# Seven 2x2-block products in place of eight for the last two blocks of each quarter of the down projection

## The chip, the cores and the metric

The kernel runs on one core of a Trainium2 chip. The metric is the device time of one execution in microseconds (us). The core's engines run side by side and meet at semaphores: TensorE (PE, with its weight loads as PEld), VectorE (DVE), ScalarE (ACT), GpSimd (POOL), and the queue of SyncE (SP), which here only issues transfers.

## The reference

One layer of a transformer-like trunk for 256 tokens of width 2048, in float32: two token mixers side by side (retention, and sliding-window attention with sinks), gated and merged, and then a feed-forward part. The change lies in the last of these lines:

```python
h2 = rms_norm(x, norm_ffn_g[l])
u = jnp.square(jax.nn.relu(jnp.einsum('bsd,df->bsf', h2, w_up[l])))
x = x + jnp.einsum('bsf,fd->bsd', u, w_down[l])
return rms_norm(x, norm_final_g)
```

`w_up` is 2048 x 8192 and `w_down` 8192 x 2048.

## The kernel before

**Blocks, units, products.** Every projection is cut into blocks of 512 output columns by 2048 rows of weight, that is 16 chunks of 128 rows. Two chunks are a unit, so a block has 8 units. The tokens are two tiles of 128. To keep float32 accuracy each factor is split into a high part in fp32r and a low part, its rest, and each product is three matmuls: high by high, high by low, low by high. One unit is thus 2 chunks x 2 tiles x 3 = 12 matmuls of 512 columns, one block is 96.

**The path of a weight block.** SP loads it into `raw` in four transfers of 1 MB (`load`, line 323; two units each). ScalarE copies each unit to `whi` (`split`, line 682), VectorE writes `raw - whi` to `wlo` (`split`, line 1016), and TensorE multiplies (`gemm`, line 431). `raw` holds one block; `whi` and `wlo` hold four units each. ScalarE's split of unit u therefore waits for TensorE to finish the unit four before it, and SP's load of slot s waits until VectorE has split both units which that slot held before. Two accumulators, `acc0` and `acc1`, take the blocks in turn.

**The order.** Nothing is scheduled by a program: each engine has its own order written out by hand. The feed-forward part is stage 6, four quarters q of the hidden width. A quarter is four up blocks (i = 0 to 3) and four down blocks (i = 4 to 7), the latter called down blocks 4 to 7 below. For a down block VectorE adds the finished accumulator to the residual `mix` (`add_residual`, line 1402) after the first three splits of the next block, and ScalarE squares the sum (`residual_squares`, line 928). The tokens' transposed activations lie in `tb_hi` and `tb_lo`. In the last quarter, down block 7 is multiplied tile by tile (`gemm_by_tile`, line 660), its upper four units are split into the free `ta_hi` and `ta_lo` (`split_last`, lines 981 and 1462), and VectorE multiplies the finished three quarters of `mix` by the final gain (line 1474) before it handles the two tiles (lines 1480 to 1491). GpSimd does nothing in stage 6 but a power of a few elements.

## Time and profile before

| | |
|---|---|
| median of 3 runs | 1485.2 us (1485.01 to 1485.22) |
| span of the profiled execution | 1483.2 us |
| PE busy | 1474.5 us, 99% |
| DVE busy | 1104.6 us, 74% |
| ACT busy | 757.7 us, 51% |
| POOL busy | 15.0 us |
| share of the chain that ended last | PE 98% |
| granted TensorE clock | 0.999 of full speed |

The span goes from the first to the last instruction of one profiled execution; its time outside the span is not given, and the median of the runs is 2.0 us above it. Busy times are of one engine each, and engines overlap. TensorE's matmuls are pipelined, so that one lasts longer than the step from one to the next.

### The profile page before, as it was taken

What the parts mean: (1) busy time and instruction counts of PE and PEld (TensorE: products, weight loads), DVE (VectorE), ACT (ScalarE), POOL (GpSimd) and SP (SyncE); (2) the same over time, 40 slices, a digit from 0 to 9 for tenths busy, and PEclk for the clock granted to TensorE, in tenths of its full rate; (3) what the DMA queues carried; (4) which work ended last, traced back from release to release, by engine and by line L of the source; (5) the groups of instructions that cost most, each with busy time, mean ns of one, the idle gap of its engine ahead of it and who ended that gap; (6) DMA issues with size and microseconds to landing.
All of it is one profiled execution on the core that took longest, in us unless ns stands there. A gap on an engine that the chain in (4) does not pass through costs nothing.

```text
span 1483.2 us, 18731 instructions
## 1 busy us (share of the span) xinstructions
PE 1474.5 (99%) x7010; PEld 1287.8 (87%) x7010; DVE 1104.6 (74%) x1448; ACT 757.7 (51%) x1009; POOL 15.0 (1%) x21
## 2 busy tenths in 40 slices
PE   9999999999999999999999999999999999999997
PEld 8888888888888888888888888888888888888886
DVE  7977887777577787777799987558865687558855
ACT  7656555444445555444454555445544555445543
POOL 0000000000000000000000000000000000000000
PEclk9999999999999999999999999999999999999999
DMA  9656555766656566556756566665566556565562
GB/s 323 199 168 216 177 164 160 230 208 241 201 170 199 182 192 221 197 193 205 253 202 221 185 201 230 206 204 174 197 229 207 191 192 226 198 203 188 200 231 86
DMA packets 149688, 299.32 MB, mean 202 GB/s; under 512 B 5120, under 2 KB 5248, under 8 KB 149376
## 3 DMA queue, kind: packets, MB, share of 16 engines
q1 hardware_dynamic: 149056, 297.51, 60.1%
q10 hardware_dynamic: 576, 1.06, 0.2%
q8 instruction: 36, 0.59, 0.2%
q14 instruction: 20, 0.16, 0.0%
HBM read 296.45 MB, written 2.10 MB: 201 GB/s over the span
## 4 chain that ended last, share of the span: by engine, by line
PE 98%; issue 1%; DVE 1%; DMA 0%; ACT 0%; POOLq 0%; POOL 0%; DVEq 0%; ACTq 0%
PE acc L431 95%; PE banks L450 1%; PE banks L469 1%; PE banks L459 0%; DMA raw<-in_w_in 0%; DVE ta_lo L1462 0%; PE banks L566 0%; PE banks L582 0%; PE banks L581 0%; PE banks L579 0%; PE acc L489 0%; DVE final L1474 0%; PE banks L567 0%; PE acc L482 0%; DVE wlo L1462 0%
## 5 line engine op out<-in xcount | busy, mean ns | idle before, releaser
L1016 DVE TENSOR_TENSOR wlo<-raw,whi 128x1024 fp32r<-128x1024 f32 x540 | 654.3, 1223 | 314.9 <-ACT whi L682 310.4
L682 ACT ACTIVATE whi<-raw 128x1024 fp32r<-128x1024 f32 x540 | 567.5, 1056 | 600.7 <-PE acc L431 597.8
L431 PE MATMUL acc<-whi,ta_hi 128*128 128x512 f32 x1308 | 497.3, 380 | 0.0
L431 PE MATMUL acc<-wlo,ta_hi 128*128 128x512 f32 x1308 | 495.7, 379 | 0.0
L431 PE MATMUL acc<-whi,ta_lo 128*128 128x512 f32 x1308 | 495.7, 379 | 0.0
L431 PE MATMUL acc<-whi,tb_hi 128*128 128x512 f32 x736 | 279.0, 379 | 0.0
L431 PE MATMUL acc<-wlo,tb_hi 128*128 128x512 f32 x736 | 278.9, 379 | 0.0
L431 PE MATMUL acc<-whi,tb_lo 128*128 128x512 f32 x736 | 278.9, 379 | 0.0
L431 PEld LDWEIGHTS acc<-whi,ta_hi 128*128 128x128 f32 x1308 | 247.2, 189 | 36.5 <-issue 1.2
L431 PEld LDWEIGHTS acc<-whi,ta_lo 128*128 128x128 f32 x1308 | 247.2, 189 | 35.1
L431 PEld LDWEIGHTS acc<-wlo,ta_hi 128*128 128x128 f32 x1308 | 247.3, 189 | 34.4
L1025 DVE STREAM_TRANSPOSE buf<-buf 32x256 f32<-32x256 f32 x384 | 167.4, 436 | 22.5 <-ACT buf L986 16.5
L431 PEld LDWEIGHTS acc<-whi,tb_hi 128*128 128x128 f32 x736 | 139.1, 189 | 20.2 <-issue 0.4
L431 PEld LDWEIGHTS acc<-wlo,tb_hi 128*128 128x128 f32 x736 | 139.1, 189 | 19.7
L431 PEld LDWEIGHTS acc<-whi,tb_lo 128*128 128x128 f32 x736 | 139.1, 189 | 19.7
L431 PE MATMUL acc<-whi,tc_hi 128*128 128x512 f32 x128 | 48.6, 380 | 0.0
L431 PE MATMUL acc<-wlo,tc_hi 128*128 128x512 f32 x128 | 48.5, 379 | 0.0
L431 PE MATMUL acc<-whi,tc_lo 128*128 128x512 f32 x128 | 48.5, 379 | 0.0
L695 ACT ACTIVATE tb_hi<-buf 128x512 fp32r<-128x512 f32 (+1 forms) x40 | 23.1, 624 | 37.0 <-DVE buf L1025 26.5
L1025 DVE STREAM_TRANSPOSE buf<-mix 32x256 f32<-32x256 f32 x64 | 27.9, 436 | 1.2
L1025 DVE STREAM_TRANSPOSE qkT<-rotated 32x256 f32<-32x256 f32 x64 | 27.9, 436 | 1.1
L1025 DVE STREAM_TRANSPOSE qT<-buf 32x256 f32<-32x256 f32 x64 | 27.9, 436 | 0.9
(158 smaller groups left out, 672.7 us busy)
## 6 DMA issues: line engine op xcount, KB each, us to landing
raw<-in_w_in SPq DMA_DIRECT2D x64, 1024.0 KB, 5.2
raw<-in_w_up SPq DMA_DIRECT2D x64, 1024.0 KB, 5.3
raw<-in_w_down SPq DMA_DIRECT2D x64, 1024.0 KB, 5.0
raw<-in_w_gate SPq DMA_DIRECT2D x32, 1024.0 KB, 5.4
raw<-in_w_att SPq DMA_DIRECT2D x16, 1024.0 KB, 5.0
raw<-in_w_ret SPq DMA_DIRECT2D x16, 1024.0 KB, 5.0
raw<-in_w_out SPq DMA_DIRECT2D x16, 1024.0 KB, 5.0
raw<-in_w_in SPq DMA_DIRECT2D x7, 512.0 KB, 9.0
```

Source lines behind the costliest of these rows:

```text
L431: last = nc.tensor.matmul(paired(acc[B.parity][:, t, :]), a[:, k, tok], halves_in_turn(b), start=(k == 0 and n == 0), stop=(k == KCH - 1 a ...
L450: last = nc.tensor.matmul(score[pair][:, h, 2 * e + m, 0:kn], qT[part, c, 2 * m:2 * m + 2, :].rearrange("p a n -> p (a n)"), keys[part, k0 ...
L469: last = nc.tensor.matmul(banks[part, pair, e, 2 * h:2 * h + 2, :].rearrange(flat), vst[:, KEYS[2 * pair + e][2], part], probT[:, pair, e, ...
L682: nc.scalar.activation(whi[:, s:s + UCH, :], raw[:, u * UCH:(u + 1) * UCH, :], ACT.Copy).then_inc(hi_ready, 1)
L695: nc.scalar.activation(dst[:, ds(g * GCH + h * UCH, UCH), :], src[:, h * UCH:(h + 1) * UCH, :], ACT.Copy).then_inc(t_hi, 1)
L1016: V_.tensor_tensor(wlo[:, s:s + UCH, :], raw[:, u * UCH:(u + 1) * UCH, :], whi[:, s:s + UCH, :].bitcast(f32), ALU.subtract).then_inc(lo_re ...
L1025: last = V_.transpose(dst(i, o), src[i:i + SQ, :, :, o:o + SQ])
```

## The change

In each quarter, the last four chunks of rows (12 to 15) of down blocks 6 and 7 form a 2 x 2 by 2 x 2 problem: two token tiles by two pairs of chunks, times two pairs of chunks by two blocks of columns. Before, its eight products of a pair of chunks by one tile by 512 columns are part of the normal blocks. Now seven such products take their place (a Strassen-Winograd form): each is 2 chunks x 3 = 6 matmuls. Called P1 to P7 in the order of `seven_products`:

- P1 and P2 are plain products of down block 6 for tile 0, P7 is one for tile 1. P4 to P6 and P3 use four combinations of the tokens (`mixed`, made by VectorE, split by ScalarE and VectorE) and three sums of weights; P6 multiplies by the plain lower chunks of block 7, and P7 by a fourth sum.
- The four sums of weights, each 128x1024, are made by GpSimd (`weight_sums`): three into `buf` 0 to 2, which ScalarE and VectorE split into `sum_hi` and `sum_lo` (`sums_hi`, `sums_lo`), and the fourth in place in `raw`, where the ordinary split of unit 1 of block 7 reads it.
- P1, P3 and P5 go on accumulating in one spare PSUM bank, `chain`. Between them VectorE adds or subtracts the bank's state to parts of `mix` (`fold`, 128x512, five per quarter), and TensorE waits for each fold before it writes the bank again.
- Block 7 loads chunks 12 to 15 first, in two transfers of 512 KB (`load_right`); its last transfer also waits for the fourth sum. The other 12 chunks are multiplied after P7 (`rest`, `rest_by_tile`).

The diff, cut to its core:

```diff
+TOP = KCH - 2 * UCH
+SUMS, MIXED, PRODUCTS, FOLDS = 3, 4, 3, 5
...
+        sum_hi = place("sum_hi", [P, SUMS, UCH, COLS], f32r, at_c)
+        sum_lo = place("sum_lo", [P, SUMS, UCH, COLS], f32r, at_c + 12 * K)
+        mixed_hi = place("mixed_hi", [P, MIXED, UCH, P], f32r, at_c + 24 * K)
+        mixed_lo = place("mixed_lo", [P, MIXED, UCH, P], f32r, at_c + 28 * K)
...
+        mixed = buf[2][:].rearrange("p t (c n) -> p (t c n)", n=P).rearrange("p (m k n) -> p m k n", m=MIXED, n=P)
+        w_sums = [b[:] for b in buf[:SUMS]]
+        left_up, left_low = raw[:, upper, :], raw[:, lower, :]
+        right_low, right_up = raw[:, 0:UCH, :], raw[:, UCH:2 * UCH, :]
...
-                for i in range(4):
+                for i in range(3):
                     load_block(Block(B6 + 4 + i, 8, q), w_down, i * COLS, q * D)
+                load_right(Block(B6 + 7, 8, q), q)
...
+            def load_right(B, q):
+                col = (GROUPS - 1) * COLS
+                parts = [w_down[ds(q * D + k * P, UCH * P), ds(col, COLS)].rearrange("(k p) n -> p k n", p=P)
+                         for k in (TOP + UCH, TOP)]
+                for src in parts:
+                    sp.lower_ap_dma(src)
+                sp.wait_ge(lo_ready, B.number * UNITS - UNITS)
+                sp.dma_start(right_low, parts[0]).then_inc(raw_full[0], 16)
+                sp.dma_start(right_up, parts[1]).then_inc(corner_full, 16)
+                for s in range(1, LOADS):
+                    if s == LOADS - 1:
+                        sp.wait_ge(sum_set, q * (SUMS + 1) + SUMS + 1)
+                    load(B, w_down[ds(q * D + (s - 1) * 512, 512), ds(col, COLS)], s)
...
+                gemm(B[5], tb_hi, tb_lo, 0, 8)
+                gemm(B[6], tb_hi, tb_lo, 0, UNITS - 2)
+                seven_products(q, B[6], B[7])
+                if last:
+                    rest_by_tile(Block(LAST))
+                else:
+                    rest(B[7])
...
+            def product(bank, left, right, start=False, stop=False, alone=True):
+                (a_hi, a_lo), (w_hi, w_lo) = left, right
+                for kk in range(UCH):
+                    for n, (a, b) in enumerate(((a_hi, w_hi), (a_hi, w_lo), (a_lo, w_hi))):
+                        done = nc.tensor.matmul(paired(bank), a[:, kk, :], halves_in_turn(b[:, kk, :]),
+                                                start=(start and kk == 0 and n == 0), stop=(stop and kk == UCH - 1 and n == 2),
+                                                skip_group_check=alone)
+                return done
+            def seven_products(q, J, K):
+                def units(k, t):
+                    return tb_hi[:, k, tokens[t]], tb_lo[:, k, tokens[t]]
+                def weights(u):
+                    s = u * UCH % (KCH // 2)
+                    return whi[:, s:s + UCH, :], wlo[:, s:s + UCH, :]
+                S1, S3, S2, S4 = [(mixed_hi[:, m], mixed_lo[:, m]) for m in range(MIXED)]
+                T1, T2, T3 = [(sum_hi[:, m], sum_lo[:, m]) for m in range(SUMS)]
+                left, right = acc[J.parity], acc[K.parity]
+                pe.wait_ge(lo_ready, J.low(UNITS - 2))
+                product(chain, units(upper, 0), weights(UNITS - 2), start=True, stop=True).then_inc(unit_done, 1)
+                pe.wait_ge(lo_ready, J.low(UNITS - 1))
+                product(left[:, 0, :], units(lower, 0), weights(UNITS - 1), stop=True, alone=False).then_inc(unit_done, 1)
+                pe.wait_ge(mixed_lo_ready, q + 1)
+                pe.wait_ge(sum_lo_ready, q * SUMS + 2)
+                pe.wait_ge(folded, q * FOLDS + 1)
+                product(chain, S2, T2, stop=True).then_inc(product_done, 1)
+                pe.wait_ge(evacuated[K.parity], K.turn)
+                product(right[:, 0, :], S1, T1, start=True, stop=True).then_inc(product_done, 1)
+                pe.wait_ge(sum_lo_ready, q * SUMS + 3)
+                pe.wait_ge(folded, q * FOLDS + 2)
+                product(chain, S3, T3, stop=True).then_inc(product_done, 1)
+                pe.wait_ge(lo_ready, K.low(0))
+                pe.wait_ge(folded, q * FOLDS + 3)
+                product(right[:, 0, :], S4, weights(0)).then_inc(unit_done, 1)
+                pe.wait_ge(lo_ready, K.low(1))
+                product(left[:, 1, :], units(lower, 1), weights(1), stop=True, alone=False).then_inc(unit_done, 1)
+            def rest_of_unit(B, u, w, tiles):
+                for kk in range(UCH):
+                    k = (u - 2) * UCH + kk
+                    for t in tiles:
+                        for n, (a, b) in enumerate(((tb_hi, w[0]), (tb_hi, w[1]), (tb_lo, w[0]))):
+                            done = nc.tensor.matmul(paired(acc[B.parity][:, t, :]), a[:, k, tokens[t]], halves_in_turn(b[:, kk, :]),
+                                                    start=(t == 1 and k == 0 and n == 0), stop=(k == TOP - 1 and n == 2),
+                                                    skip_group_check=True)
+                return done
+            def rest(B):
+                for u in range(2, UNITS):
+                    pe.wait_ge(lo_ready, B.low(u))
+                    s = u * UCH % (KCH // 2)
+                    rest_of_unit(B, u, (whi[:, s:s + UCH, :], wlo[:, s:s + UCH, :]), range(TILES)).then_inc(unit_done, 1)
...
+                split(B[5], 0, 5)
+                residual_squares(B[4], 0, down_sq)
+                act.wait_ge(mixed_set, q * MIXED + MIXED)
+                nc.scalar.activation(mixed_hi[:], mixed, ACT.Copy).then_inc(mixed_hi_ready, 1)
+                split(B[5], 5, 8)
+                split(B[6], 0, 5)
+                residual_squares(B[5], 1, down_sq)
+                sums_hi(q, 0)
+                sums_hi(q, 1)
+                split(B[6], 5, 6)
+                sums_hi(q, 2)
+                split(B[6], 6, 8)
+                if last:
+                    split_last(B[7], 0, 1)
+                    act.wait_ge(sum_set, q * (SUMS + 1) + SUMS + 1)
+                    split_last(B[7], 1, UNITS)
+                    residual_squares(B[6], 2, down_sq)
+                else:
+                    split(B[7], 0, 1)
+                    act.wait_ge(sum_set, q * (SUMS + 1) + SUMS + 1)
+                    split(B[7], 1, 5)
+                    residual_squares(B[6], 2, down_sq)
+                    split(B[7], 5, 8)
+            def sums_hi(q, m):
+                act.wait_ge(sum_set, q * (SUMS + 1) + m + 1)
+                nc.scalar.activation(sum_hi[:, m], w_sums[m], ACT.Copy).then_inc(sum_hi_ready, 1)
...
+                split(B[5], 0, 3)
+                if not first:
+                    dve.wait_ge(down_sq, q * 4 - 3)
+                add_residual(B[4], 0)
+                split(B[5], 3, 4)
+                mixed_tokens(q)
+                split(B[5], 4, 6)
+                dve.wait_ge(mixed_hi_ready, q + 1)
+                V_.tensor_tensor(mixed_lo[:], mixed, mixed_hi[:].bitcast(f32), ALU.subtract).then_inc(mixed_lo_ready, 1)
+                split(B[5], 6, 8)
+                split(B[6], 0, 3)
+                if not first:
+                    dve.wait_ge(down_sq, q * 4 - 2)
+                add_residual(B[5], 1)
+                split(B[6], 3, 4)
+                split(B[6], 4, 5)
+                sums_lo(q, 0)
+                split(B[6], 5, 6)
+                sums_lo(q, 1)
+                split(B[6], 6, 8)
+                sums_lo(q, 2)
+                last_part = split_last if last else split
+                last_part(B[7], 0, 1)
+                if not first:
+                    dve.wait_ge(down_sq, q * 4)
+                dve.wait_ge(unit_done, B[6].unit(UNITS - 2))
+                fold(0, 2, chain, ALU.add)
+                last_part(B[7], 1, 2)
+                dve.wait_ge(product_done, q * PRODUCTS + 1)
+                fold(0, 3, chain, ALU.subtract)
+                dve.wait_ge(product_done, q * PRODUCTS + 2)
+                fold(1, 3, acc[B[7].parity][:, 0, :], ALU.add)
+                last_part(B[7], 2, 3)
+                dve.wait_ge(product_done, q * PRODUCTS + 3)
+                dve.wait_ge(folded, q * FOLDS + 3)
+                fold(1, 3, chain, ALU.subtract)
+                fold(1, 2, chain, ALU.add)
+                last_part(B[7], 3, 4)
+                dve.wait_ge(folded, q * FOLDS + FOLDS)
+                dve.wait_ge(unit_done, B[7].unit(1))
+                add_residual(B[6], 2)
+                last_part(B[7], 4, 8)
...
+            def mixed_tokens(q):
+                dve.wait_ge(t_full, q * 4 + (T_STAGE6 + 4))
+                (a11, a21), (a12, a22) = [[turned[:, half, tokens[t]] for t in range(TILES)] for half in (slice(0, UCH), slice(UCH, GCH))]
+                V_.tensor_tensor(mixed[:, 0], a21, a22, ALU.subtract).then_inc(mixed_set, 1)
+                V_.tensor_tensor(mixed[:, 1], a11, a21, ALU.subtract).then_inc(mixed_set, 1)
+                dve.wait_ge(mixed_set, q * MIXED + 1)
+                V_.tensor_tensor(mixed[:, 2], mixed[:, 0], a11, ALU.subtract).then_inc(mixed_set, 1)
+                dve.wait_ge(mixed_set, q * MIXED + 3)
+                V_.tensor_tensor(mixed[:, 3], mixed[:, 2], a12, ALU.add).then_inc(mixed_set, 1)
+            def sums_lo(q, m):
+                dve.wait_ge(sum_hi_ready, q * SUMS + m + 1)
+                V_.tensor_tensor(sum_lo[:, m], w_sums[m], sum_hi[:, m].bitcast(f32), ALU.subtract).then_inc(sum_lo_ready, 1)
+            def fold(t, j, bank, how):
+                sl = by_half(mix[:, t, j * COLS:(j + 1) * COLS])
+                V_.tensor_tensor(sl, sl, unpaired(bank), how).then_inc(folded, 1)
...
+            def weight_sums(q):
+                J, K = Block(B6 + 6, 8, q), Block(B6 + 7, 8, q)
+                pool.wait_ge(mixed_lo_ready, q + 1)
+                pool.wait_ge(t_free, q * 4 + (T_STAGE6 + 4))
+                pool.wait_ge(raw_full[LOADS - 1], J.number * 16 + 16)
+                pool.wait_ge(corner_full, q * 16 + 16)
+                nc.gpsimd.tensor_tensor(w_sums[0], left_up, right_up, ALU.add).then_inc(sum_set, 1)
+                pool.wait_ge(raw_full[0], K.number * 16 + 16)
+                pool.wait_ge(sum_set, q * (SUMS + 1) + 1)
+                nc.gpsimd.tensor_tensor(w_sums[1], w_sums[0], right_low, ALU.add).then_inc(sum_set, 1)
+                nc.gpsimd.tensor_tensor(w_sums[2], right_up, right_low, ALU.add).then_inc(sum_set, 1)
+                pool.wait_ge(sum_set, q * (SUMS + 1) + 3)
+                nc.gpsimd.tensor_tensor(right_up, w_sums[1], left_low, ALU.add).then_inc(sum_set, 1)
```
```

`rest_by_tile` runs `rest_of_unit` for one tile after the other, `split_last` takes its first and last unit as arguments, and `weight_sums` is called for all four quarters.

VectorE's rows of the last quarter from the fourth split of down block 5 to the end of the splits, before (L1016, L1462 the splits, L1402 the residual of a block):

```order
L1016 TENSOR_TENSOR wlo<-raw,whi 128x1024 [waits hi_ready] x8
L1402 TENSOR_TENSOR mix<-mix,acc 128x2x512 [waits unit_done,down_sq]
L1016 TENSOR_TENSOR wlo<-raw,whi 128x1024 [waits hi_ready] x5
L1462 TENSOR_TENSOR wlo<-raw,whi 128x1024 [waits hi_ready] x4
L1462 TENSOR_TENSOR ta_lo<-raw,ta_hi 128x1024 [waits hi_ready] x4
```

The same place on VectorE now, from the residual of down block 5 on (L1122 and L1621 the splits, L1611 `sums_lo`, L1615 `fold`, L1508 the residual):

```order
L1508 TENSOR_TENSOR mix<-mix,acc 128x2x512 [waits unit_done,down_sq]
L1122 TENSOR_TENSOR wlo<-raw,whi 128x1024 [waits hi_ready] x2
L1611 TENSOR_TENSOR sum_lo<-buf_59,sum_hi 128x1024 [waits sum_hi_ready]
L1122 TENSOR_TENSOR wlo<-raw,whi 128x1024 [waits hi_ready]
L1611 TENSOR_TENSOR sum_lo<-buf_60,sum_hi 128x1024 [waits sum_hi_ready]
L1122 TENSOR_TENSOR wlo<-raw,whi 128x1024 [waits hi_ready] x2
L1611 TENSOR_TENSOR sum_lo<-buf_61,sum_hi 128x1024 [waits sum_hi_ready]
L1621 TENSOR_TENSOR wlo<-raw,whi 128x1024 [waits hi_ready]
L1615 TENSOR_TENSOR mix<-mix,banks 128x512 [waits unit_done,down_sq]
L1621 TENSOR_TENSOR wlo<-raw,whi 128x1024 [waits hi_ready]
L1615 TENSOR_TENSOR mix<-mix,banks 128x512 [waits product_done]
L1615 TENSOR_TENSOR mix<-mix,acc 128x512 [waits product_done]
```

Three subtractions for the sums now stand among the last splits of block 6, and the first fold behind the first split of block 7; two more folds and the residual of block 6 follow.

GpSimd's rows of one quarter, of which it had none before, between its last two powers:

```order
L1672 TENSOR_TENSOR rstd_74<-msq,mhalf 128x2 [waits ms2_ready]
L1680 TENSOR_TENSOR buf_59<-raw 128x1024 [waits raw_full3,corner_full,t_free,mixed_lo_ready]
L1683 TENSOR_TENSOR buf_60<-buf_59,raw 128x1024 [waits sum_set,raw_full0]
L1684 TENSOR_TENSOR buf_61<-raw 128x1024
L1686 TENSOR_TENSOR raw<-buf_60,raw 128x1024 [waits sum_set]
```

Each of these four has two operands in SBUF (a row names a tensor once), and each but the third waits for one before it.

## Rows read from the trace of the kernel before

**Rows 1.** The page: busy time by engine, and the chain by engine and line.

```profile
PE 1474.5 (99%) x7010; PEld 1287.8 (87%) x7010; DVE 1104.6 (74%) x1448; ACT 757.7 (51%) x1009; POOL 15.0 (1%) x21
...
PE acc L431 95%; PE banks L450 1%; PE banks L469 1%; PE banks L459 0%; DMA raw<-in_w_in 0%; DVE ta_lo L1462 0%; PE banks L566 0%; PE banks L582 0%; PE banks L581 0%; PE banks L579 0%; PE acc L489 0%; DVE final L1474 0%; PE banks L567 0%; PE acc L482 0%; DVE wlo L1462 0%
```

**Rows 2.** Timeline of PE: start, length, engine, line, tiles.

```profile
1433.86 0.38 PE L431 MATMUL acc<-whi,tb_lo 128*128 128x512 f32 x1
1434.08 0.38 PE L431 MATMUL acc<-whi,tb_hi 128*128 128x512 f32 x1
```

**Rows 3.** Busy time in three stretches: an up block, down blocks 5 and 6.

```profile
core 0: us, PE busy (x) PEld busy (x) DVE busy (x) ACT busy (x) POOL busy (x), PEclk, DMA share, GB/s
1391.00:1411.70 20.70, 20.70 (x98) 18.12 (x97) 17.70 (x27) 11.58 (x14) 0.00 (x0) 1.00 0.60 210
1413.37:1434.08 20.71, 20.71 (x97) 18.14 (x96) 10.93 (x9) 9.68 (x12) 0.00 (x0) 1.00 0.67 226
1434.08:1454.80 20.72, 20.72 (x97) 18.14 (x96) 10.93 (x9) 9.68 (x12) 0.00 (x0) 1.00 0.56 185
```

**Rows 4.** Timeline of ACT, last quarter, early in down block 6.

```profile
1436.93 1.06 ACT L682 ACTIVATE whi<-raw 128x1024 fp32r<-128x1024 f32 x1 [1.59 <-PE acc L431]
1437.89 0.62 ACT L928 ACTIVATE buf<-mix 128x512 f32<-128x512 f32 x1
```

**Rows 5.** Timeline of DVE: two operands of 256 elements.

```profile
29.73 0.42 DVE L1214 TENSOR_TENSOR buf<-xsq 128x256 f32<-128x256 f32 x1
```

**Rows 6.** Timeline of DVE, last quarter, around the start of block 6.

```profile
1430.19 1.22 DVE L1016 TENSOR_TENSOR wlo<-raw,whi 128x1024 fp32r<-128x1024 f32 x1 [1.30 <-ACT whi L682]
...
1434.35 1.22 DVE L1402 TENSOR_TENSOR mix<-mix,acc 128x1024 f32<-128x1024 f32 x1 [0.29 <-PE acc L431]
1435.49 1.22 DVE L1016 TENSOR_TENSOR wlo<-raw,whi 128x1024 fp32r<-128x1024 f32 x1
1438.02 1.23 DVE L1016 TENSOR_TENSOR wlo<-raw,whi 128x1024 fp32r<-128x1024 f32 x1 [1.31 <-ACT whi L682]
```

**Rows 7.** Transfers into raw, 1380 to 1448 us, from issue to landing.

```profile
DMA to landing us min/median/max: 4.9/5.1/5.6
```

**Rows 8.** Timeline of POOL: its copies in stage 1.

```profile
50.25 1.37 POOL L1505 COPY keys<-kT 128x256 f32<-128x256 f32 x1 [13.34 <-DVE kT L1025]
51.57 1.50 POOL L1508 COPY vst<-vwin 128x384 f32<-128x384 f32 x1
64.33 0.52 POOL L1505 COPY keys<-kT 128x256 f32<-128x256 f32 x1 [11.26 <-PE banks L450]
...
111.78 0.40 POOL L1505 COPY keys<-kT 128x256 f32<-128x256 f32 x1 [14.37 <-PE banks L450]
144.09 0.76 POOL L1508 COPY vst<-vwin 128x384 f32<-128x384 f32 x1 [31.91 <-PE banks L469]
```

**Rows 9.** Timeline of DVE at the same times.

```profile
50.14 2.56 DVE L1016 TENSOR_TENSOR wlo<-raw,whi 128x1024 fp32r<-128x1024 f32 x2
...
62.23 2.35 DVE L1016 TENSOR_TENSOR wlo<-raw,whi 128x1024 fp32r<-128x1024 f32 x2
...
111.46 1.02 DVE L1132 TENSOR_REDUCE mx<-banks 128x4 f32<-128x256 f32 x2
...
143.26 1.22 DVE L1016 TENSOR_TENSOR wlo<-raw,whi 128x1024 fp32r<-128x1024 f32 x1 [1.37 <-ACT whi L682]
```

**Rows 10.** Line 1016 from 49 to 54 us: shortest, median, longest.

```profile
L1016 DVE TENSOR_TENSOR wlo<-raw,whi x2: 1224/1322/1419, 50.1 to 51.3; 128x1024 fp32r<-128x1024 f32 x2
```

**Rows 11.** Timeline of DVE at the end.

```profile
1463.12 3.36 DVE L1474 TENSOR_TENSOR final<-mix,gfin 128x3072 f32<-128x3072 f32 x1
1466.39 0.68 DVE L1480 TENSOR_TENSOR mix<-mix,acc 128x512 f32<-128x512 f32 x1
...
1475.72 0.69 DVE L1480 TENSOR_TENSOR mix<-mix,acc 128x512 f32<-128x512 f32 x1 [5.83 <-PE acc L660]
```

More of the change, by code:

```diff
@@ L221, in build @@
         out_ps = tps.rearrange("p (i t) e -> p i t e", t=TILES)
+        chain = rs_ps[1]
         raw_full = [sem(f"raw_full{s}") for s in range(LOADS)]
@@ L654, in gemm_by_tile @@
                         if t == 0:
                             pe.wait_ge(lo_ready, B.low(u))
[L656 to L661 removed]
+                        done = rest_of_unit(B, u, [last_slot(part, u) for part in range(2)], (t,))
@@ L1446, in stage6 @@
                     split(B[i], 7, 8)
-                for i in range(5, 8):
-                    if i == 7 and last:
-                        split_last(B[i])
-                    else:
-                        split(B[i], 0, 3)
-                    if not first:
-                        dve.wait_ge(down_sq, q * 4 + (i - 8))
-                    add_residual(B[i - 1], i - 5)
-                    if i < 7 or not last:
-                        split(B[i], 3, 8)
-            def split_last(B):
-                for u in range(UNITS):
+                split(B[5], 0, 3)
```

41 lines of the change are left out of this document (15 added, 26 removed).

## Prediction

> **What bounds the kernel now.** The page comes first. TensorE is busy for 99% of the span, and 95% of the chain that ended last is the matmuls of line 431 [rows 1]. So a matmul that goes is worth its full step, and anything that holds TensorE up costs its full length. The timeline gives the step: one matmul starts at 1433.86 and the next at 1434.08 [rows 2]. The windows give it more finely: a block of 96 takes 20.71 us [rows 3], 0.216 us each, 2.59 us per unit and 1.29 us per product of six. In that table the engines that would have to do the new work have room: during a down block VectorE is busy 10.93 of 20.71 us, ScalarE 9.68, GpSimd not at all; only in up blocks is VectorE nearly full (17.70 of 20.70). The question is when the new work ends. For that I read the timelines of VectorE and ScalarE at the start of down block 6, called T (1434.08 in the last quarter).
>
> **What goes.** One product of eight per quarter: 6 x 0.216 = 1.29 us, four times, **5.2 us**. No matmul of a product differs in shape from the old ones.
>
> **What is added and hidden.** ScalarE gets four copies of 1.06 us (one for the tokens, three for the sums) beside its 9.68 us per block; the squares of a block cost it 2 x 0.6 and two short reads [rows 4]. It stays ahead unless it waits for a sum. In block 5 VectorE makes the four token combinations at 0.42 us each, by the nearest form [rows 5], and one subtraction of 1.22 us, 2.9 us in all against 9.8 us of idle time. I cost these at nothing; without that idle time they would be 2.9 us per quarter. The lead that covers them: VectorE's split of unit 3 of block 6 begins 1.41 us after T [rows 6], ends at T+2.6, and is needed at T+7.8, 5.1 us later.
>
> **When the sums can start.** The transfer of chunks 12 to 15 of block 7 is issued when unit 1 of block 6 is split, which is at 1430.19 + 1.22 = 1431.41 = T-2.7 [rows 6]. A 1 MB transfer lands 5.1 us after its issue [rows 7]; two halves one behind the other should end at the same moment, T+2.4. The sums need both halves, so GpSimd starts at T+2.5. The second issue delays SP by well under 1 us. The later transfers of block 7 follow VectorE's splits as before; the last one also waits for the fourth sum, which is done before VectorE frees its slot anyway.
>
> **What GpSimd and VectorE do to each other.** GpSimd's copies of stage 1 are the only ones beside VectorE's splits. Alone, beside a reduction, the 256-element copy takes 0.40 us [rows 8, 9]. At 50.25 it takes 1.37: a split had begun at 50.14 and the next begins 1.14 us later (back to back, such operations step by 1.14, from 1434.35 to 1435.49 [rows 6]), at 51.28. 51.28 + 0.34 is the copy's end. At 64.33 it takes 0.52, and the two splits from 62.23 end their reading at about 64.5. The copy at 144.09 (0.76) and the one at 51.57 (1.50) end 0.45 and about 0.4 us after a split has made way. So a GpSimd instruction waits for a whole two-operand subtraction of VectorE. The other way round there is one case: the split from 51.28, behind the delayed copy, took 1.419 in place of 1.224 us [rows 10], 0.2 us for some 0.34 us of copy. I take it that they exclude each other, with an operation that has two operands in SBUF on VectorE. The Trainium skill says the same more strongly (SBUF — State Buffer, "SBUF: two separate sides"): the shared pair of ports is an exclusive lock, held for the full instruction, against a VectorE operation with two SBUF inputs when GpSimd reads SBUF. By that rule, with which the trace agrees for GpSimd's waits (four of them) and only weakly for VectorE's (one, 0.2 us), the result is the forecast; without it 1480.5.
>
> **How long a weight sum takes.** No row shows one; call it s. Lower end: the longest copy, 384 elements in 0.45 us of its own, scaled to 1024 gives 1.2 us. Upper end: 256 elements in 0.40 us, scaled to 1024 and doubled for two operands, 3.2 us. A fixed part in both copies makes scaling too dear, the second operand makes the lower end too cheap, and neither end is nearer; I take the middle, **s = 2.2 us**. The Trainium skill (GPSIMD Engine Reference, "Performance versus the Vector engine") has 4497 ns for a 2048-element add; half of it, 2.25 us, would be an estimate from that page and would move the result to 1494.5.
>
> **The path to the first fold.** From T+2.5 on, VectorE must do eight subtractions with two SBUF operands before the first fold, by the new order: splits 4 to 7 of block 6, the three `sums_lo`, split 0 of block 7. At a step of 1.15 us these are 9.2 us. Four sums stand between them, since they feed those very subtractions. Who goes first matters little: the first fold starts at T + 2.5 + 9.2 + 4s = T+20.5. It takes 0.68 us, as the same form does in the tail [rows 11], and the way to TensorE and a weight load cost about 0.2 (189 ns is one weight load's busy time: 18.14 us over 96 [rows 3]), so P3 starts at T+21.4. Undisturbed it would start at T + 6 x 2.59 + 2 x 1.29 = T+18.1. That is 3.3 us of idle TensorE per quarter, generally **4s - 5.5**: about 1.8 ahead of P1, which waits for split 6 (T + 2.5 + 8.8 + 5 x 1.15 + 0.3 = T+17.4 against 15.5), and the rest ahead of P3, which waits for the fold.
>
> After P3 the folds fit: a finished matmul is seen by VectorE 0.27 us after the next could start (1434.08 to 1434.35 [rows 2, 6]), plus 0.68 of fold and 0.2 back is 1.15 against a product's 1.29. That is only 0.14 of slack, three times a quarter.
>
> In the last quarter TensorE takes a unit of block 7 every 1.29 us, for one tile. VectorE comes out of the folds late: the residual of block 6, then the split of unit 4 is done about 3.1 us after P7, needed at 2.6: **0.5 us** more. The 3.36 us multiply [rows 11] that follows is over before tile 1 is (tile 0's old lead was 1475.72 - 1466.39 = 9.3 us), so the tail stays.
>
> **Sum.** Per quarter 3.3 - 1.29 = +2.0; four of them and the 0.5 are +8.5. The profiled span of 1483.2 becomes 1491.7; the runs lay 2.0 us above the span, so the time is **1493.7 us**. What a measurement can tell from no change is 0.2%, 3 us.
>
> **Rivals.**
>
> *A, forecast (0.58):* sums and subtractions exclude each other and s is 1.9 to 2.6; 4 x (4s - 6.8) + 0.5 gives +3.7 to +14.9, 1489 to 1500. For it: the four delayed copies [rows 8, 9].
>
> *B, the other side (0.24):* VectorE loses only part of a sum's length, as the one slowed split suggests (0.2 for 0.34), or s is near its lower end. The point that decides is an effective s of 1.37 us: below it there is no idle time, and the time is 1485.2 - 5.2 + 0.5 = 1480.5. At 0.6 of 2.2 us, s is 1.3.
>
> *C, in between (0.13):* effective s of 1.5 to 1.85, where the idle time eats what the product saves; within 3 us of before, 1482 to 1488. The same comes of B with the three later folds each 0.3 us late: 1480.5 + 4 x 3 x 0.3 = 1484.1.
>
> *D (0.05):* s of 3.2, the two operands read one after the other: 4 x 6.0 + 0.5 = +24.5, 1509.7. VectorE would be held up while it still has splits 4 and 5 to make, and TensorE would stop inside block 6 too.
>
> A product that doesn't go is no case: the new order has 42 matmuls for 48.
>
> **How the numbers follow.** The likeliest case is A, and the predicted time its sum. Its own range is 1489 to 1500. The range that holds 8 in 10 takes in C and most of B, whose time is known well: 1480.5 to 1500. Faster by over 0.2% is B, 0.24; same is C, 0.13; slower is A and D, 0.63.
>
> **What would show it.** In the profile after: 24 fewer matmuls; four GpSimd sums per quarter, beginning 2.5 us after block 6 does, each 2.2 us plus what it waits for a split; VectorE splits and subtractions of over 2 us among them, that is 1.2 and a sum's length; TensorE idle for 1.8 us before P1 and 1.5 before P3, four times; nothing before P5 to P7. Splits that stay at 1.22 us beside the sums would refute A and leave B. Idle TensorE before P5 or P6 would be the folds' own lateness, idle within block 6 case D, and an idle time before P6's plain weights or block 7's late units a transfer that I costed at nothing.

## The result, and the profile after

| | before | after |
|---|---|---|
| median of 4 runs | 1485.19 us | 1493.62 us (1493.03 to 1494.24) |
| span of the profiled execution | 1483.2 us | 1491.8 us |
| matmuls | 7010 | 6986 |
| PE / DVE / ACT / POOL busy | 1474.5 / 1104.6 / 757.7 / 15.0 us | 1472.1 / 1163.5 / 771.7 / 63.6 us |
| granted TensorE clock | 0.999 | 0.999 |

The ratio is 1.0056, with a 95% interval of 1.0043 to 1.0069: slower by 8.4 us. The 24 matmuls have gone, and the time has still grown.

The page of the changed kernel, as in [rows 1]: busy time by engine, then the chain that ended last by engine and by line.

```profile
PE 1472.1 (99%) x6986; PEld 1282.7 (86%) x6986; DVE 1163.5 (78%) x1500; ACT 771.7 (52%) x1025; POOL 63.6 (4%) x37
...
PE 91%; DVE 3%; issue 3%; DMA 1%; POOL 1%; ACT 1%; POOLq 0%; DVEq 0%; SPq 0%; ACTq 0%
PE acc L465 83%; PE acc L731 3%; DVE wlo L1122 1%; DMA raw<-in_w_down 1%; PE acc L689 1%; DVE sum_lo L1611 1%; POOL buf L1683 1%; PE banks L689 1%; ACT whi L770 1%; PE banks L484 1%; PE banks L503 1%; PE banks L493 0%; POOL buf L1680 0%; PE banks L511 0%; DVE ta_lo L1621 0%
```

L465 is `gemm`, L689 `product`, L1122 VectorE's split, L1611 `sums_lo`, L1680 and L1683 GpSimd's sums. TensorE's share of the chain has fallen from 98 to 91%. VectorE and GpSimd have 3 and 1% of it now, and "issue" (time in which the profile shows nothing that was waited for) has 3% where it had 1.

The timeline of GpSimd in the last quarter (start, length, engine, line, tiles). Down block 6 begins at T = 1440.24 there:

```profile
1442.98 2.38 POOL L1680 TENSOR_TENSOR buf<-raw 128x1024 f32<-128x1024 f32 x1 [155.45 <-DMA raw<-in_w_down]
1445.51 3.17 POOL L1683 TENSOR_TENSOR buf<-buf,raw 128x1024 f32<-128x1024 f32 x1
1448.64 3.36 POOL L1684 TENSOR_TENSOR buf<-raw 128x1024 f32<-128x1024 f32 x1
1452.07 3.25 POOL L1686 TENSOR_TENSOR raw<-buf,raw 128x1024 f32<-128x1024 f32 x1
```

The first sum starts at T+2.7 and takes 2.38 us alone. The other three last 3.2 to 3.4 us, because each waits for an operation of VectorE. The starts and lengths in the other three quarters are the same within 0.2 us.

The timeline of VectorE over the same stretch; 1440.52 is the residual that [rows 6] have at 1434.35:

```profile
1440.52 1.22 DVE L1508 TENSOR_TENSOR mix<-mix,acc 128x1024 f32<-128x1024 f32 x1 [0.29 <-PE acc L465]
1441.65 1.22 DVE L1122 TENSOR_TENSOR wlo<-raw,whi 128x1024 fp32r<-128x1024 f32 x1
1444.18 2.26 DVE L1122 TENSOR_TENSOR wlo<-raw,whi 128x1024 fp32r<-128x1024 f32 x1 [1.31 <-ACT whi L770]
1446.49 3.27 DVE L1611 TENSOR_TENSOR sum_lo<-buf,sum_hi 128x1024 fp32r<-128x1024 f32 x1
1450.75 2.33 DVE L1122 TENSOR_TENSOR wlo<-raw,whi 128x1024 fp32r<-128x1024 f32 x1 [0.99 <-ACT whi L770]
1453.00 3.40 DVE L1611 TENSOR_TENSOR sum_lo<-buf,sum_hi 128x1024 fp32r<-128x1024 f32 x1
1456.33 2.35 DVE L1122 TENSOR_TENSOR wlo<-raw,whi 128x1024 fp32r<-128x1024 f32 x2
1458.60 1.21 DVE L1611 TENSOR_TENSOR sum_lo<-buf,sum_hi 128x1024 fp32r<-128x1024 f32 x1
1459.74 1.21 DVE L1621 TENSOR_TENSOR wlo<-raw,whi 128x1024 fp32r<-128x1024 f32 x1
1460.88 0.67 DVE L1615 TENSOR_TENSOR mix<-mix,banks 128x512 f32<-128x512 f32 x1
```

Before, these splits were 1.22 us long. Beside the sums one takes 2.26, one 2.33, and two `sums_lo` take 3.27 and 3.40. A row that starts behind a running sum ends about 1.1 us after the sum does: the sum from 1442.98 ends at 1445.36 and the split from 1444.18 at 1446.44. Once the last sum is over (1455.32), the subtractions are back at about 1.2 us each and VectorE runs without a pause to the first fold, at 1460.88 = T+20.6.

TensorE's timeline, the first matmul of block 6 and those around the two pauses:

```profile
1440.24 0.38 PE L465 MATMUL acc<-whi,tb_hi 128*128 128x512 f32 x1
...
1455.61 0.38 PE L465 MATMUL acc<-whi,tb_lo 128*128 128x512 f32 x1
1457.60 0.48 PE L689 MATMUL banks<-whi,tb_hi 128*128 128x512 f32 x1 [1.61 <-DVE wlo L1122]
...
1460.08 0.38 PE L689 MATMUL acc<-whi,tb_lo 128*128 128x512 f32 x1
1461.70 0.45 PE L689 MATMUL banks<-sum_hi,mixed_hi 128*128 128x512 f32 x1 [1.24 <-DVE mix L1615]
```

P1 starts at T+17.4 and P3 at T+21.5. Nothing waits between P3 and the end of P7. The two pauses cost 3.3 us in this quarter (P3 at T+21.46, and T+18.12 without them) and 3.2 to 3.3 in the others.

### The profile page after: what moved, and what is told of

Read it like the earlier page. It is cut to its first block, busy times and chain, and to the rows that moved or that the text cites. A ratio compares the mean times of both kernels' runs of the same rounds, so it can differ in the third digit from the quotient of the medians.

```text
span 1491.8 us, 18850 instructions
## 1 busy us (share of the span) xinstructions
PE 1472.1 (99%) x6986; PEld 1282.7 (86%) x6986; DVE 1163.5 (78%) x1500; ACT 771.7 (52%) x1025; POOL 63.6 (4%) x37
## 3 DMA queue, kind: packets, MB, share of 16 engines
q10 hardware_dynamic: 576, 1.06, 0.2%
## 4 chain that ended last, share of the span: by engine, by line
PE 91%; DVE 3%; issue 3%; DMA 1%; POOL 1%; ACT 1%; POOLq 0%; DVEq 0%; SPq 0%; ACTq 0%
PE acc L465 83%; PE acc L731 3%; DVE wlo L1122 1%; DMA raw<-in_w_down 1%; PE acc L689 1%; DVE sum_lo L1611 1%; POOL buf L1683 1%; PE banks L689 1%; ACT whi L770 1%; PE banks L484 1%; PE banks L503 1%; PE banks L493 0%; POOL buf L1680 0%; PE banks L511 0%; DVE ta_lo L1621 0%
## 5 line engine op out<-in xcount | busy, mean ns | idle before, releaser
L1122 DVE TENSOR_TENSOR wlo<-raw,whi 128x1024 fp32r<-128x1024 f32 x540 | 661.7, 1238 | 268.2 <-ACT whi L770 263.8
L770 ACT ACTIVATE whi<-raw 128x1024 fp32r<-128x1024 f32 x540 | 566.3, 1056 | 576.6 <-PE acc L465 530.5
L465 PE MATMUL acc<-whi,ta_hi 128*128 128x512 f32 x1308 | 497.3, 380 | 0.0
L465 PE MATMUL acc<-wlo,ta_hi 128*128 128x512 f32 x1308 | 495.7, 379 | 0.0
L465 PE MATMUL acc<-whi,ta_lo 128*128 128x512 f32 x1308 | 495.7, 379 | 0.0
L465 PEld LDWEIGHTS acc<-whi,ta_hi 128*128 128x128 f32 x1308 | 247.2, 189 | 36.3 <-issue 1.2
L465 PEld LDWEIGHTS acc<-whi,ta_lo 128*128 128x128 f32 x1308 | 247.2, 189 | 35.1
L465 PEld LDWEIGHTS acc<-wlo,ta_hi 128*128 128x128 f32 x1308 | 247.3, 189 | 34.6
L465 PE MATMUL acc<-whi,tb_hi 128*128 128x512 f32 x608 | 230.7, 379 | 0.0
L465 PE MATMUL acc<-wlo,tb_hi 128*128 128x512 f32 x608 | 230.4, 379 | 0.0
L465 PE MATMUL acc<-whi,tb_lo 128*128 128x512 f32 x608 | 230.4, 379 | 0.0
L465 PEld LDWEIGHTS acc<-whi,tb_hi 128*128 128x128 f32 x608 | 114.9, 189 | 17.1 <-DVE wlo L1122 0.4
L465 PEld LDWEIGHTS acc<-whi,tb_lo 128*128 128x128 f32 x608 | 114.9, 189 | 16.3
L465 PEld LDWEIGHTS acc<-wlo,tb_hi 128*128 128x128 f32 x608 | 114.9, 189 | 16.2
L465 PE MATMUL acc<-whi,tc_hi 128*128 128x512 f32 x128 | 48.6, 380 | 0.0
L465 PE MATMUL acc<-wlo,tc_hi 128*128 128x512 f32 x128 | 48.5, 379 | 0.0
L465 PE MATMUL acc<-whi,tc_lo 128*128 128x512 f32 x128 | 48.5, 379 | 0.0
L1680 POOL TENSOR_TENSOR buf<-raw 128x1024 f32<-128x1024 f32 x4 | 9.5, 2377 | 574.3 <-DMA raw<-in_w_down 574.3
L1611 DVE TENSOR_TENSOR sum_lo<-buf,sum_hi 128x1024 fp32r<-128x1024 f32 x12 | 31.5, 2628 | 0.2
L731 PE MATMUL acc<-whi,tb_hi 128*128 128x512 f32 x80 | 30.3, 379 | 0.0
```

What stands on the lines that cost most here:

```text
L465: last = nc.tensor.matmul(paired(acc[B.parity][:, t, :]), a[:, k, tok], halves_in_turn(b), start=(k == 0 and n == 0), stop=(k == KCH - 1 a ...
L731: done = nc.tensor.matmul(paired(acc[B.parity][:, t, :]), a[:, k, tokens[t]], halves_in_turn(b[:, kk, :]), start=(t == 1 and k == 0 and n ...
L770: nc.scalar.activation(whi[:, s:s + UCH, :], raw[:, u * UCH:(u + 1) * UCH, :], ACT.Copy).then_inc(hi_ready, 1)
L1122: V_.tensor_tensor(wlo[:, s:s + UCH, :], raw[:, u * UCH:(u + 1) * UCH, :], whi[:, s:s + UCH, :].bitcast(f32), ALU.subtract).then_inc(lo_re ...
L1611: V_.tensor_tensor(sum_lo[:, m], w_sums[m], sum_hi[:, m].bitcast(f32), ALU.subtract).then_inc(sum_lo_ready, 1)
L1680: nc.gpsimd.tensor_tensor(w_sums[0], left_up, right_up, ALU.add).then_inc(sum_set, 1)
```

## The experiments

Each kernel was timed beside the kernel before on the same chip.

**e1: the sums are made, but nobody waits for the first three.** ScalarE and VectorE split other resident data, so the mixed products are left out of the result.

```diff
-                act.wait_ge(sum_set, q * (SUMS + 1) + m + 1)
-                nc.scalar.activation(sum_hi[:, m], w_sums[m], ACT.Copy)
+                nc.scalar.activation(sum_hi[:, m], other, ACT.Copy)
...
-                nc.gpsimd.tensor_tensor(right_up, w_sums[1], left_low, ALU.add)
+                nc.gpsimd.tensor_tensor(w_sums[0], w_sums[1], left_low, ALU.add)
```

> The changed kernel, but nothing waits for the first three weight sums: ScalarE and VectorE split other resident data in their place, and the fourth sum is written to a buffer that nobody reads (so the down projection is wrong by the mixed products). GpSimd still makes all four sums at the same place. Theory (sums and VectorE's two-operand subtractions exclude each other): the same eight subtractions and four sums stand before the first fold, so 1492 to 1494 us, P1 at T+17.4 and P3 at T+21.4 again. Rival (the sums are simply late, and TensorE waits for them through ScalarE's copies): without anybody waiting for them the idle time goes, 1480.5 us.

1493.58 us, ratio 1.0057 (1.0041 to 1.0072). TensorE's waits in the changed kernel (engine, line, waited for: total us, times, longest):

```profile
PE banks L689 <- DVE wlo L1122: 6.3, 4, 1.6
PE banks L689 <- DVE mix L1615: 4.8, 4, 1.2
```

and in e1:

```profile
PE banks L690 <- DVE wlo L1122: 6.1, 4, 1.6
PE banks L690 <- DVE mix L1615: 4.8, 4, 1.2
```

They are the same waits. A late delivery of the first three sums is not the cause; the fourth is needed only for P7, before which nothing waits. What GpSimd does to VectorE by working beside it is enough.

**e2 and e5: GpSimd at work, but only writing.** Each sum is replaced by memsets of its target, three (e2) or two (e5). Together they last longer (2.97 us) or shorter (1.96 us) than a sum alone (2.38 us). The sums are constants, so the kernel leaves out the products that need them.

```diff
-                nc.gpsimd.tensor_tensor(w_sums[0], left_up, right_up, ALU.add).then_inc(sum_set, 1)
+                fill(w_sums[0])
+                nc.gpsimd.memset(w_sums[0], 1.0).then_inc(sum_set, 1)
```

> The changed kernel with each weight sum replaced by three memsets of its 128x1024 target, one after the other (the sums are constants then, so the mixed products are wrong); all waits stay. GpSimd is as long in giving the sums, but reads nothing from SBUF. Theory (GpSimd's reads and VectorE's second operand exclude each other): no split is stretched beyond 1.3 us, no idle time at P1 and P3, 1480.5 us, as long as three memsets take no more than 2.6 us together. Rival (the sums are late as such): three memsets of 2.4 us in all give 1493 us again. Rival (GpSimd's writes exclude VectorE as well): splits of about 2 us and 1488 to 1494 us.

1484.49 us, ratio 0.9994 (0.9984 to 1.0003), 9 us below the changed kernel. GpSimd's first "sum" in the last quarter, its two fills and its last memset:

```profile
1436.23 1.96 POOL L1679 MEMSET buf<- 128x1024 f32 x2 [153.46 <-DMA raw<-in_w_down]
1438.25 0.95 POOL L1690 MEMSET buf<- 128x1024 f32 x1
```

and VectorE beside it, the split of unit 4, the first `sums_lo` and the split of unit 5:

```profile
1437.47 1.23 DVE L1123 TENSOR_TENSOR wlo<-raw,whi 128x1024 fp32r<-128x1024 f32 x1 [1.31 <-ACT whi L771]
1440.32 1.23 DVE L1612 TENSOR_TENSOR sum_lo<-buf,sum_hi 128x1024 fp32r<-128x1024 f32 x1 [1.63 <-ACT sum_hi L1079]
1444.36 1.23 DVE L1123 TENSOR_TENSOR wlo<-raw,whi 128x1024 fp32r<-128x1024 f32 x1 [2.81 <-ACT whi L771]
```

None is stretched. The time lies above the 1480.5 expected, and the rows say why: three memsets take 2.97 us, so the second sum reaches ScalarE at 1442.33, and in its fixed order the split of unit 5 stands behind it; VectorE idles 2.81 us. The first fold comes at T+18.3, and TensorE waits 0.8 us before P3 in the profile's count (0.9 to 1.0 by the steps of its matmuls), four times. This is the rival's lateness at 2.97 us per sum. e5 checks it:

> As the run with three memsets per sum, but with two, about 1.96 us per sum. There three memsets took 2.97 us and the first fold still came at T+18.3, behind sums handed over late, with no split stretched. Theory (what excludes is GpSimd's reading; its length counts only for when a sum is handed over): no idle time at P3, 1480.2 to 1480.6 us. Rival (some other cost of GpSimd's work beside VectorE): stays at 1482 us or more.

1479.92 us, ratio 0.9964 (0.9951 to 0.9977). No time is left over. e2 has taken the stretching away and e5 the lateness too, so what costs is that GpSimd reads. Its sums read two operands; whether one would do, as with the copies of stage 1 [rows 8], was not tried here.

**e3: the kernel before with four idle additions per quarter.**

```diff
+            for q in range(4):
+                idle_sums(q)
...
+                    nc.gpsimd.tensor_tensor(idle_out[dst % 2][:], idle_a[:], idle_b[:], ALU.add).then_inc(idle_set, 1)
```

> The kernel before, with four GpSimd additions of 128x1024 that nobody uses in each quarter's down block 6, from the split of its unit 3 on. Theory: VectorE's splits beside them take about 2.3 us in place of 1.22, but block 6 has only 8 splits and a residual (10.9 us) beside 9 us of additions in 20.7 us and VectorE keeps most of its 5 us of lead, so TensorE never waits: 1485.2 us within 0.3. If GpSimd cost TensorE or the transfers something of its own: above 1486 us.

1485.19 us, ratio 1.000 (0.9991 to 1.0009); one of its ten runs took 1487.23, the others 1484.9 to 1485.5. GpSimd, four additions merged into one row:

```profile
1436.99 12.33 POOL L1521 TENSOR_TENSOR idle<-idle,idle 128x1024 f32<-128x1024 f32 x4 [153.52 <-DVE wlo L1018]
```

and VectorE's splits of units 4 to 7 beside them:

```profile
1438.22 2.23 DVE L1018 TENSOR_TENSOR wlo<-raw,whi 128x1024 fp32r<-128x1024 f32 x1 [1.31 <-ACT whi L684]
1440.75 9.65 DVE L1018 TENSOR_TENSOR wlo<-raw,whi 128x1024 fp32r<-128x1024 f32 x3 [0.30 <-ACT whi L684]
```

The exclusion is there in full (2.23 us, then three in 9.65), and it costs nothing: block 6 has room for some 9 us of additions beside 10.9 us of VectorE's work. It is the sum of GpSimd's additions and VectorE's new work that does not fit.

**e4: all four sums on VectorE.** This is the changed kernel with the smallest edit that takes GpSimd out.

```diff
                 split(B[6], 3, 4)
+                V_.tensor_tensor(w_sums[0], left_up, right_up, ALU.add).then_inc(sum_set, 1)
+                V_.tensor_tensor(w_sums[1], w_sums[0], right_low, ALU.add).then_inc(sum_set, 1)
                 split(B[6], 4, 5)
+                V_.tensor_tensor(w_sums[2], right_up, right_low, ALU.add).then_inc(sum_set, 1)
+                V_.tensor_tensor(right_up, w_sums[1], left_low, ALU.add).then_inc(sum_set, 1)
                 sums_lo(q, 0)
```

> The changed kernel with the four weight sums of a quarter made by VectorE itself (two before and two behind the split of unit 4 of block 6), GpSimd idle. Theory: a sum then takes 1.15 us of VectorE's time in place of 2.2 us of exclusion, the first fold could start at T + 2.6 + 12 x 1.15 = T+16.4, before P1 ends (T+17.1), so nothing waits: 1485.2 - 5.2 + 0.2 to 0.5 = 1480.2 to 1480.5 us, faster than both. Rival (the seven products themselves cost TensorE something at the folds, or the rearranged loads do): 1483 us or more with idle time before P3, P5 or P6.

1480.18 us (1479.99 to 1480.35), ratio 0.9966 (0.9952 to 0.9979): 5.3 us below the kernel before, and it computes the same. VectorE in the last quarter, the first sum, then the split of block 7's unit 0 and the first fold (block 6 began at 1430.05):

```profile
1432.79 1.23 DVE L1571 TENSOR_TENSOR buf<-raw 128x1024 f32<-128x1024 f32 x1
...
1445.60 1.22 DVE L1630 TENSOR_TENSOR wlo<-raw,whi 128x1024 fp32r<-128x1024 f32 x1
1447.15 0.69 DVE L1624 TENSOR_TENSOR mix<-mix,banks 128x512 f32<-128x512 f32 x1 [0.34 <-PE banks L689]
```

The sums take 1.23 us each. VectorE is done with everything ahead of the fold at T+16.8 and idles 0.34 us until P1 ends. TensorE loses no time before P1 to P7 in any quarter; in all of stage 6 it stops once, for 0.2 us before unit 4 of the last block 7.

**e6: the fourth sum on VectorE, three on GpSimd.**

```diff
-                nc.gpsimd.tensor_tensor(right_up, w_sums[1], left_low, ALU.add).then_inc(sum_set, 1)
...
                 sums_lo(q, 2)
+                V_.tensor_tensor(right_up, w_sums[1], left_low, ALU.add).then_inc(sum_set, 1)
```

> The changed kernel with the fourth weight sum made by VectorE behind the last sums_lo, the other three by GpSimd. Theory (sums and subtractions add up): the first fold starts at T + 2.5 + 3 x 2.2 + 9 x 1.15 = T+19.5, P1 waits for nothing (split 6 at T+15.2), P3 starts at T+20.3 in place of 18.1; per quarter 2.2 - 1.3 = +0.9, in all 1485.2 + 3.9 = 1489.1 us (1488.3 to 1490). Rival (one waits for the last sum as such, whichever engine makes it): 1493 us again.

1490.98 us, ratio 1.0037 (1.0023 to 1.0050), 1 us above the expected range. The times lie far apart: 1488.82, 1490.69, 1490.98, 1492.59, 1492.61. The first fold starts at T+19.6 and P3 at T+20.4, as the sum had them, and the lowest run is where it was expected. In the profiled run, one of 1492.61, the rest comes from TensorE's clock. Three-us windows of TensorE in the first quarter (columns as in [rows 3], for TensorE alone):

```profile
core 0: us, PE busy (x), PEclk, DMA share, GB/s
953.00:956.00 3.00, 2.25 (x11) 1.00 0.41 158
956.00:959.00 3.00, 1.70 (x6) 0.84 0.81 236
959.00:962.00 3.00, 3.00 (x10) 0.59 1.01 357
962.00:965.00 3.00, 3.00 (x16) 1.00 0.28 107
```

and the matmuls in them, the last of P2 and the first of P3:

```profile
954.88 0.38 PE L689 MATMUL acc<-whi,tb_lo 128*128 128x512 f32 x1
957.30 0.45 PE L689 MATMUL banks<-sum_hi,mixed_hi 128*128 128x512 f32 x1 [2.05 <-DVE mix L1617]
...
958.42 0.63 PE L689 MATMUL banks<-sum_lo,mixed_hi 128*128 128x512 f32 x1
958.84 0.63 PE L689 MATMUL banks<-sum_hi,mixed_lo 128*128 128x512 f32 x1
```

TensorE stood idle from 955.10 to 957.30, ran three matmuls in 0.73 us, and from 958.03 took up to 0.43 us for each until 961.66: nine steps for 3.63 us instead of 1.94, 1.7 us more. The windows show the granted clock at 0.84 and 0.59 over stretches that hold the fall and the recovery; a step twice as long is the 1.2 GHz level. In this execution it happened in two of four quarters. The runs at 1488.8, about 1490.8 and about 1492.6 are about 1.9 us apart, as none, one and two such falls would give; that is an inference, since only one of them has a trace.

**e7: the first fold ahead of the split of block 7.**

```diff
-                last_part(B[7], 0, 1)
...
                 fold(0, 2, chain, ALU.add)
-                last_part(B[7], 1, 2)
+                last_part(B[7], 0, 1)
                 dve.wait_ge(product_done, q * PRODUCTS + 1)
                 fold(0, 3, chain, ALU.subtract)
+                last_part(B[7], 1, 2)
```

> The changed kernel with VectorE's first fold ahead of the split of block 7's unit 0, and the second fold ahead of the split of unit 1; the sums stay on GpSimd. Theory: P1 waits as before (1.8 us), the first fold no longer has that split in front of it, so P3 waits 0.3 us in place of 1.5, and P6 waits 0.3 us for the later folds; per quarter +1.2, in all 1485.2 + 5.2 = 1490.4 us (1489.5 to 1491.3). Rival (P3 waits for its weight sums and not for the fold's place in VectorE's order): 1493 us again.

1490.37 us, ratio 1.0033 (1.0020 to 1.0047), on the forecast. VectorE's last `sums_lo`, and the first fold directly behind it:

```profile
1455.74 1.21 DVE L1611 TENSOR_TENSOR sum_lo<-buf,sum_hi 128x1024 fp32r<-128x1024 f32 x1
1456.88 0.67 DVE L1615 TENSOR_TENSOR mix<-mix,banks 128x512 f32<-128x512 f32 x1
```

TensorE's pause before P1 is still 1.6 us in the profile's count, as in the changed kernel. The one before P3 is no longer in that count: by the steps of the matmuls it is 0.2 to 0.3 us (1457.22 to 1457.70 in the last quarter, where a step is 0.216), against 1.3 to 1.4 before. P6 now waits 0.1 to 0.2 us, where I expected 0.3. Most of the second pause belonged to the fold's place in VectorE's queue, and the first to split 6.

**e8: the residual of block 6 later, in the last quarter.** e4 with `add_residual(B[6], 2)` behind the last four splits of the last quarter.

> The version with all sums on VectorE, and in the last quarter the residual of block 6 behind the last four splits of block 7 in place of ahead of them. In the version without this TensorE shows no idle time of note between P7 and the end, so both theories say 1480.2 us within 0.3: no gain is left there.

1480.18 us, ratio 0.9964 (0.9951 to 0.9978), the same as e4. TensorE's 0.2 us before unit 4 of the last block 7 are gone from its rows, and the time doesn't move: nothing is left there.

**e9: third and fourth sum on VectorE.** Besides the two sums, ScalarE's copy of the third now stands between its splits of units 6 and 7.

> The changed kernel with the third and fourth weight sums made by VectorE (behind the second sums_lo, and ahead of the split of block 7's unit 0), the first two by GpSimd. Theory: the first fold starts at T + 2.5 + 2 x 2.2 + 10 x 1.15 = T+18.4, P3 at T+19.3; 1.2 us of idle time per quarter against 1.3 saved: 1485.0 us (1484.2 to 1485.8). Second question: with three sums on GpSimd there were idle times of 2.4 us, and behind them the granted clock fell to half for some 3 us in some quarters; behind 1.2 us it should stay at 1.00, and the runs should lie within 0.6 us of each other, not 3.8.

1496.95 us, ratio 1.0079 (1.0061 to 1.0097). This expectation was wrong by 12 us. ScalarE in the last quarter, its copy of the third sum and the split of unit 7 behind it:

```profile
1456.14 1.06 ACT L1078 ACTIVATE sum_hi<-buf 128x1024 fp32r<-128x1024 f32 x1 [2.62 <-DVE buf L1574]
1457.10 1.04 ACT L770 ACTIVATE whi<-raw 128x1024 fp32r<-128x1024 f32 x1
```

VectorE, the third sum, the split of unit 6 and the one of unit 7:

```profile
1454.88 1.22 DVE L1574 TENSOR_TENSOR buf<-raw 128x1024 f32<-128x1024 f32 x1
1456.02 1.22 DVE L1122 TENSOR_TENSOR wlo<-raw,whi 128x1024 fp32r<-128x1024 f32 x1
1458.17 1.22 DVE L1122 TENSOR_TENSOR wlo<-raw,whi 128x1024 fp32r<-128x1024 f32 x1 [0.93 <-ACT whi L770]
```

In my order ScalarE waits 2.6 us for a sum that VectorE makes late, and then VectorE waits 0.9 us for ScalarE's split that stands behind it; another pause of 1.0 us stands before the split of unit 5. So P2 waits up to 0.4 us in the profile's count for the split of unit 7 besides. The first fold comes at T+20.4, TensorE idles 2.7 us before P3 (1460.85 to 1463.54), and the clock falls in the profile's first and last quarter. By the steps of the matmuls the waits are 3.2 to 3.4 us per quarter in place of 1.2, some 8 us in all, and the two falls add 1.7 us each. I had counted the operations and not the crossing of two in-order queues.

**e10: sums of half the columns** (the other half of each sum is left out).

```diff
-                nc.gpsimd.tensor_tensor(w_sums[0], left_up, right_up, ALU.add).then_inc(sum_set, 1)
+                nc.gpsimd.tensor_tensor(w_sums[0][:, :, 0:COLS // 2], left_up[:, :, 0:COLS // 2], right_up[:, :, 0:COLS // 2], ALU.add).then_inc(sum_set, 1)
```

> The changed kernel with GpSimd summing only the first 256 of the 512 columns of each of the four weight sums (the other half of each sum is left out, so the mixed products are wrong). Theory: a sum of 128x512 takes about 1.2 us by itself and excludes VectorE for 1.1, below the 1.37 us from which TensorE begins to wait: 1480.2 to 1480.8 us, splits beside a sum about 1.2 + 1.0 = 2.2 us at most, most of them under 2. Rival (a sum's cost is mostly fixed per instruction): 1.8 us or more each, 1485 us or more.

1480.71 us, ratio 0.9970 (0.9958 to 0.9982). GpSimd's first two sums:

```profile
1433.14 1.29 POOL L1680 TENSOR_TENSOR buf<-raw 128x512 f32<-128x512 f32 x1 [156.45 <-DMA raw<-in_w_down]
1434.57 2.20 POOL L1683 TENSOR_TENSOR buf<-buf,raw 128x512 f32<-128x512 f32 x1
```

and on VectorE the longest `sums_lo` and the first fold:

```profile
1440.00 2.30 DVE L1611 TENSOR_TENSOR sum_lo<-buf,sum_hi 128x1024 fp32r<-128x1024 f32 x1
...
1447.57 0.69 DVE L1615 TENSOR_TENSOR mix<-mix,banks 128x512 f32<-128x512 f32 x1 [0.73 <-PE banks L689]
```

Alone a sum of 512 elements takes 1.29 us against 2.38 for 1024, so little of it is fixed. VectorE is still held up (2.30 us), but it waits 0.73 us for P1 before the first fold: with so little of it the exclusion is free, as in e3.

**e11: two sums on each engine, in another order.** VectorE makes the third sum directly behind the split of block 6's unit 3 and the fourth behind the second `sums_lo`.

> Once more two weight sums on each of the two engines, in an order in which ScalarE's copies and VectorE's subtractions don't wait for each other: VectorE makes the third sum directly behind its split of block 6's unit 3, and the fourth behind the second sums_lo; ScalarE's order is that of the changed kernel. In the earlier try VectorE stood idle for 1 us before each of two splits, the first fold began at T+20.4 in place of T+18.4, TensorE stood idle for 2.9 us before P3 and the granted clock fell behind it. Theory: without these waits the first fold starts at T + 2.5 + 2 x 2.2 + 10 x 1.15 = T+18.4, P3 at T+19.3, 1.2 us of idle time per quarter against 1.3 saved: 1485.0 us (1484.0 to 1486.0), clock 1.00. Rival (two-engine sums cost more than their exclusion): 1489 us or more.

1486.86 us, ratio 1.0010 (1.0001 to 1.0020), clock 0.999, runs within 0.6 us. Ten us are gone against e9, so e9's excess was its order and the falls of the clock that it brought. But the time is 1.9 us above the expectation. VectorE, the split of unit 5 and the first fold (T = 1434.94):

```profile
1446.50 1.23 DVE L1126 TENSOR_TENSOR wlo<-raw,whi 128x1024 fp32r<-128x1024 f32 x1 [0.99 <-ACT whi L771]
...
1454.45 0.68 DVE L1625 TENSOR_TENSOR mix<-mix,banks 128x512 f32<-128x512 f32 x1
```

VectorE idles 0.99 us before unit 5, because ScalarE's split of it stands behind a copy that waits for GpSimd's second sum. The fold comes at T+19.5 and not T+18.4. The first quarter is like it; in the two middle ones the pause is absent, the fold comes at T+18.5 and T+18.7, and TensorE idles 1.2 and 1.4 us, as expected. The difference is which engine comes first when the data lands: in the first and last quarter VectorE's sum, so that GpSimd's first takes 3.32 us, in the middle ones GpSimd's (2.38). Two quarters of four, about 0.8 and 1.0 us late, make up the 1.9 us. The changed kernel has the same 0.99 us in its rows (1450.75); there GpSimd's third sum runs under it, so it costs nothing.

## Why the prediction was right

Forecast 1493.7 us, measured 1493.62; the span was to be 1491.7 and is 1491.8. The steps, one by one:

- **What goes:** 5.2 us. e4 and e5 get 5.3 and 5.4 us out of the change once nothing waits before P1 or P3. Right, and it holds for all of the seven products: the later folds fit into their 0.14 us of slack, and TensorE does not wait before P5 or P6 but in e7, where the order is another (0.1 to 0.2 us before P6).
- **When the sums start:** forecast T+2.5, measured T+2.7. The two half transfers land about 0.2 us later than I had one land.
- **That they exclude each other:** right. The strongest evidence is e1 (nobody waits for the first three sums, same time), e2 and e5 (durations above and below a sum's, no reading, no stretched split). The weak point was the one slowed split of before (0.2 us for 0.34 of copy); behind a sum a split now loses about 1.0 us, all of the time it had to wait. The rule of the Trainium skill (SBUF — State Buffer, "SBUF: two separate sides"), an exclusive lock for the full instruction, agrees with e3's rows (2.23 us for a split that takes 1.22), up to the small difference told below. The same page of the Trainium skill, "Who interferes with whom", has it that a GpSimd instruction that only writes does not contend; e2's splits at 1.23 us beside memsets agree.
- **s = 2.2 us:** a sum takes 2.38 alone. The idle time of 3.34 us in the last quarter (P3 at T+21.46 against T+18.12) put into 4s - 5.5 gives s = 2.21 as what it takes from VectorE. The value was the middle of two far ends, so that its nearness is partly luck. The figure of the Trainium skill (GPSIMD Engine Reference, "Performance versus the Vector engine") for 2048 elements, halved to an estimate of 2.25, is 0.13 below the measured 2.38.
- **P1 at T+17.4 and P3 at T+21.4:** measured T+17.4 and T+21.5.
- **0.5 us in the last quarter:** too much. TensorE waits 0.2 us for unit 4 of block 7, and the step after that is 0.1 longer; VectorE has that unit split 2.7 us after P7 and not 3.1. The pauses of the four quarters add up to 13.1 us, where the sum had 13.2, and what goes is 0.1 to 0.2 us above its 5.2. With misses of this size and runs that spread over 1.2 us, a total within 0.1 us is in part luck.
- **The line 4s - 5.5 as a law:** only right where VectorE has no pause of its own. With four and three sums on GpSimd its one pause lay under a sum (first fold at T+20.6 and T+19.6, computed 20.5 and 19.5). With two it misses by about 1 us in two quarters of e11 and by 2 in e9.

The bound of rival B held in e10: with sums of half the size, below an effective s of 1.37 us, TensorE waits nowhere before P1 to P7, and 4.6 of the 5.2 us are there. Case D did not come up.

That P1's pause hangs on split 6 and P3's on the fold is shown by e7, which removes most of the second alone. The rows of the changed kernel also show the turns: while both have work, one instruction of each follows the other. GpSimd's sums end at 1448.68, 1452.00 and 1455.32, each 2.24 us after VectorE's row before it (1446.44, 1449.76, 1453.08), and VectorE's rows end 1.08 us after each sum. So a sum under contention takes 2.24 us of the shared time, less than its 2.38 alone. Whether some part of a sum leaves VectorE free was not tried; that difference hints at it and no more.
